# Wide matmuls in a two-layer and one-block transformer kernel: both halves of a feature tile in one pass of 512 columns

## The reference

```python
h = h + g1 * y                                    # y = even_mixer(...) @ w_out, or pool_mix(...)
hn = modulate(rms_norm(h, norm_ffn_g[layer]), sh2, sc2)
h = h + g2 * swiglu(hn, w1, w3, w2)               # hidden width 2816, two layers
...
x = x + mix @ w_out                               # second block, after DeltaNet and sparse attention
h2 = rmsnorm(x, norm_mlp)
x = x + jnp.square(jax.nn.relu(h2 @ w_up)) @ w_down   # hidden width 4096
```

## Time and profile before

| | |
|---|---|
| Median of three runs | 1388.35 us |
| Profiled execution, its own time | 1396.09 us |
| Its span | 1394.3 us |
| Mean granted TensorE clock | 0.945 |
| TensorE matmul busy | 1271.6 us (91%), 9480 records |
| TensorE weight load busy | 1180.4 us (85%), 9480 records |
| VectorE busy | 930.1 us (67%), 1562 records |
| ScalarE busy | 650.3 us (47%), 1163 records |
| GpSimd busy | 314.2 us (23%), 155 records |

### The profile page before, as it was taken

How to read it: one execution, slowest core, us unless ns; L and a number is a source line. 1 busy time by engine, 2 the same in 40 slices (tenths; PEclk the granted TensorE clock), 3 DMA queues, 4 the chain that set the end, 5 groups by cost and what they waited for, 6 DMA issues and landing times.

```text
span 1394.3 us, 22620 instructions
## 1 busy us (share of the span) xinstructions
PE 1271.6 (91%) x9480; PEld 1180.4 (85%) x9480; DVE 930.1 (67%) x1562; ACT 650.3 (47%) x1163; POOL 314.2 (23%) x155
## 2 busy tenths in 40 slices
PE   5679889999987999997997897988999999899999
PEld 1676679999976999996987775767999899899999
DVE  4956768998767665444476886777754576677543
ACT  2535746666545554433533445454322455465432
POOL 0241123433200100000732433331553530000000
PEclk9899999999989999996997998979999999999999
DMA  9642637888742656412351211112201265665530
GB/s 392 239 187 65 248 139 299 320 321 324 308 181 105 262 214 236 159 63 96 122 204 68 65 64 54 61 61 65 87 1 46 102 209 181 231 205 206 191 103 12
DMA packets 32358, 226.52 MB, mean 162 GB/s; under 512 B 3584, under 2 KB 4736, under 8 KB 5120
## 3 DMA queue, kind: packets, MB, share of 16 engines
q1 hardware_dynamic: 30528, 221.20, 42.9%
q10 hardware_dynamic: 1728, 3.87, 0.8%
HBM read 224.01 MB, written 1.05 MB: 161 GB/s over the span
## 4 chain that ended last, share of the span: by engine, by line
PE 73%; DVE 18%; ACT 7%; issue 1%; DMA 1%; POOL 0%; SPq 0%; DVEq 0%; POOLq 0%; ACTq 0%
PE bank L515 20%; PE bank L516 19%; PE bank L517 19%; PE bank L535 2%; ACT sb_whi L1140 2%; PE bank L1038 2%; PE bank L1025 2%; DVE sb_qk L2076 1%; DVE sb_tmp L1629 1%; DVE sb_bk L1923 1%; PE bank L1034 1%; ACT sb_ss L1423 1%; DVE sb_qk L2064 1%; DVE sb_qk L2088 1%; PE bank L820 1%
## 5 line engine op out<-in xcount | busy, mean ns | idle before, releaser
L515 PE MATMUL bank<-sb_xh,sb_whi 128*128 128x256 f32 x1544 | 453.5, 294 | 35.5 <-DVE sb_xl L1634 19.4
L516 PE MATMUL bank<-sb_xl,sb_whi 128*128 128x256 f32 x1544 | 442.6, 287 | 0.0
L517 PE MATMUL bank<-sb_xh,sb_wlo 128*128 128x256 f32 x1544 | 441.9, 286 | 0.0
L515 PEld LDWEIGHTS bank<-sb_xh,sb_whi 128*128 128x128 f32 x1544 | 303.3, 196 | 51.3 <-issue 19.0
L516 PEld LDWEIGHTS bank<-sb_xl,sb_whi 128*128 128x128 f32 x1544 | 304.4, 197 | 0.5 <-issue 0.2
L517 PEld LDWEIGHTS bank<-sb_xh,sb_wlo 128*128 128x128 f32 x1544 | 302.4, 196 | 0.0
L1140 ACT ACTIVATE sb_whi<-sb_ring 128x1024 fp32r<-128x1024 f32 (+1 forms) x201 | 210.5, 1050 | 92.6 <-PE bank L517 82.0
L1610 DVE TENSOR_TENSOR sb_wlo<-sb_ring,sb_whi 128x1024 fp32r<-128x1024 f32 x145 | 186.4, 1291 | 94.3 <-ACT sb_whi L1140 94.0
L2276 POOL TENSOR_TENSOR sb_wlo<-sb_ring,sb_whi 128x1024 fp32r<-128x1024 f32 x56 | 134.6, 2416 | 356.6 <-ACT sb_whi L1140 356.6
L1610 DVE TENSOR_TENSOR sb_wlo<-sb_more,sb_whi 128x1024 fp32r<-128x1024 f32 x108 | 145.2, 1352 | 72.6 <-ACT sb_whi L1140 72.3
L515 PE MATMUL bank<-sb_hh,sb_whi 128*128 128x256 f32 x608 | 174.2, 287 | 0.0
(11 more groups left out here) (337 smaller groups left out, 2247.5 us busy)
## 6 DMA issues: line engine op xcount, KB each, us to landing
sb_more<-in_w SPq DMA_DIRECT2D x34, 1024.0 KB, 5.3
sb_ring<-in_w SPq DMA_DIRECT2D x32, 1024.0 KB, 5.1
sb_ring<-in_adaT SPq DMA_DIRECT2D x26, 1024.0 KB, 7.2
sb_ring<-in_f SPq DMA_DIRECT2D x24, 1024.0 KB, 4.9
sb_more<-in_adaT SPq DMA_DIRECT2D x18, 1024.0 KB, 8.2
sb_ring<-in_gn SPq DMA_DIRECT2D x8, 1024.0 KB, 4.9
sb_ring<-in_gd SPq DMA_DIRECT2D x8, 1024.0 KB, 4.9
sb_ring<-in_up SPq DMA_DIRECT2D x8, 1024.0 KB, 4.9
```

The lines of the kernel that those rows point to most:

```text
L515: te.matmul(out, wh, rh, start=start, stop=False, skip_group_check=skip)
L516: te.matmul(out, wh, rl, start=False, stop=False, skip_group_check=skip)
L517: return te.matmul(out, wl, rh, start=False, stop=stop, skip_group_check=skip)
```

## The change

Each pair of high and low data becomes one tile in which the two halves of a feature tile lie side by side, 512 columns. The new helper `mm_wide` multiplies the high weights by both at once into the whole bank, and the low weights by the high data into its first 256 columns. So the bank holds two partial sums, and `residual` adds them to `h` one after the other, the second waiting for the first. The pool stage keeps its single one (`wide=False`). For every weight tile the wide matmul is issued first and the narrow one second; for the last weight tile of a group the order is turned round, so that the wide one ends it.

```diff
--- before.py
+++ after.py
@@ -361,16 +361,16 @@
         xcl = sb("xcl", [128, KT, T], F32R)
         kT = sb("kT", [128, 2, T])
         qT = sb("qT", [128, 4, T])
-        ah = sb("ah", [128, 8, T], F32R)
-        al = sb("al", [128, 8, T], F32R)
+        ahl = sb("ahl", [128, 8, 2, T], F32R)
+        ah, al = ahl[:, :, 0, :], ahl[:, :, 1, :]
         v0 = sb("v0", [128, 2, 2, 128])
         SBs = sb("SBs", [128, 10, T])
         PTs = ctxr[:, 0:6, :]
         close()
 
         scope()
-        hh = sb("hh", [128, NH0, T], F32R)
-        hl = sb("hl", [128, NH0, T], F32R)
+        hhl = sb("hhl", [128, NH0, 2, T], F32R)
+        hh, hl = hhl[:, :, 0, :], hhl[:, :, 1, :]
         more[1] = sb("more", [128, NEXTRA, SLOT])
         z8 = sb("z8", [128, 8, T])
         close()
@@ -420,8 +420,8 @@
         Msb = sb("Msb", [128, 4, 512])
         close()
         scope()
-        mxh = sb("mxh", [128, 8, T], F32R)
-        mxl = sb("mxl", [128, 8, T], F32R)
+        mxx = sb("mxx", [128, 8, 2, T], F32R)
+        mxh, mxl = mxx[:, :, 0, :], mxx[:, :, 1, :]
         odh = sb("odh", [128, 8, T], F32R)
         odl = sb("odl", [128, 8, T], F32R)
         close()
@@ -430,8 +430,8 @@
 
         scope()
         more[2] = sb("more2", [128, NEXTRA, SLOT])
-        hh2 = sb("hh2", [128, NH2, T], F32R)
-        hl2 = sb("hl2", [128, NH2, T], F32R)
+        hhl2 = sb("hhl2", [128, NH2, 2, T], F32R)
+        hh2, hl2 = hhl2[:, :, 0, :], hhl2[:, :, 1, :]
         close()
 
         def K(name, lo=0, hi=None):
@@ -515,6 +515,27 @@
                 te.matmul(out, wh, rh, start=start, stop=False, skip_group_check=skip)
                 te.matmul(out, wh, rl, start=False, stop=False, skip_group_check=skip)
                 return te.matmul(out, wl, rh, start=False, stop=stop, skip_group_check=skip)
+
+            def mm_wide(ps, wh, wl, r, first, last):
+
+                x = r.rearrange("p e t -> p (e t)")
+                if not last:
+                    te.matmul(ps[:, :], wh, x, start=first, stop=False, skip_group_check=True)
+                end = te.matmul(ps[:, 0:T], wl, r[:, 0, :], start=False, stop=last, skip_group_check=True)
+                if last:
+                    end = te.matmul(ps[:, :], wh, x, start=first, stop=True, skip_group_check=True)
+                return end
+
+            def product_wide(n, r, ready, ps):
+
+                _, hi, lo = unit_of(n)
+                P.wait_ge(*lo_done(n))
+                for k in range(KT):
+                    P.wait_ge(*dve.at(ready, k))
+                    c = slice(k * 128, (k + 1) * 128)
+                    end = mm_wide(ps, hi[:, c], lo[:, c], r[:, k, :, :], k == 0, k == KT - 1)
+                F.done(n)
+                return end
 
             def product(n, rh, rl, ready, out):
 
@@ -677,7 +698,7 @@
             for j in range(8):
                 u, _ = F.take("mixout")
                 ps = take(RG, ("mo", j), (dve, ("h", "ffn0", j)))
-                product(u, ah, al, "a", ps[:, 0:T]).then_inc(*pe.up(("mo", j), ("unit", u)))
+                product_wide(u, ahl, "a", ps).then_inc(*pe.up(("mo", j), ("unit", u)))
                 if j > 0:
                     mean_square("ffn0", j - 1)
             mean_square("ffn0", 7)
@@ -708,7 +729,7 @@
                             P.wait_ge(*lo_done(u))
                         P.wait_ge(*dve.at("hid", layer, k))
                         c = slice((n % 8) * 128, (n % 8 + 1) * 128)
-                        end = mm3(ps[:, 0:T], hi[:, c], lo[:, c], hh[:, k, :], hl[:, k, :], k == 0, k == NH0 - 1)
+                        end = mm_wide(ps, hi[:, c], lo[:, c], hhl[:, k, :, :], k == 0, k == NH0 - 1)
                         steps = [("unit", u)] * (n % 8 == 7) + [("down", layer, j)] * (k == NH0 - 1)
                         if steps:
                             end.then_inc(*pe.up(*steps))
@@ -1090,7 +1111,7 @@
             for j in range(8):
                 u, _ = F.take("wout2")
                 ps = take(RG, ("res", j), (dve, ("h", "mlp2", j)))
-                product(u, mxh, mxl, "mx", ps[:, 0:T]).then_inc(*pe.up(("res", j), ("unit", u)))
+                product_wide(u, mxx, "mx", ps).then_inc(*pe.up(("res", j), ("unit", u)))
                 if j > 0:
                     mean_square("mlp2", j - 1)
             mean_square("mlp2", 7)
@@ -1112,7 +1133,7 @@
                         P.wait_ge(*lo_done(u))
                     P.wait_ge(*dve.at("mhid", k))
                     c = slice((n % 8) * 128, (n % 8 + 1) * 128)
-                    end = mm3(ps[:, 0:T], hi[:, c], lo[:, c], hh2[:, k, :], hl2[:, k, :], k == 0, k == NH2 - 1)
+                    end = mm_wide(ps, hi[:, c], lo[:, c], hhl2[:, k, :, :], k == 0, k == NH2 - 1)
                     if n % 8 == 7:
                         end.then_inc(*pe.up(("unit", u), ("mdown", j)) if k == NH2 - 1 else pe.up(("unit", u)))
                         F.done(u)
@@ -1662,10 +1683,14 @@
             def scaled(i, gain, scale):
                 ve.scalar_tensor_tensor(scl[:, i, :], scale, 1.0, gain, ALU.add, ALU.mult).then_inc(*dve.up())
 
-            def residual(norm, j, step, gate):
-                V.wait_ge(*pe.at(step, j) if isinstance(step, str) else pe.at(*step, j))
-                ve.scalar_tensor_tensor(h[:, j, :], ps_of((step, j) if isinstance(step, str) else (*step, j))[:, 0:T], gate, h[:, j, :],
-                                        ALU.mult, ALU.add).then_inc(*dve.up(("h", norm, j)))
+            def residual(norm, j, step, gate, wide=True):
+
+                V.wait_ge(*pe.at(*step))
+                for e in range(1 + wide):
+                    if e:
+                        V.wait_ge(*dve.now())
+                    ve.scalar_tensor_tensor(h[:, j, :], ps_of(step)[:, e * T:(e + 1) * T], gate, h[:, j, :], ALU.mult, ALU.add).then_inc(
+                        *dve.up(*[("h", norm, j)] * (e == wide)))
 
 
             V.wait_ge(s_col, 16)
@@ -1775,7 +1800,7 @@
             for j in range(8):
                 weights("mixout")
                 V.wait_ge(*m2)
-                residual("ffn0", j, "mo", mods[:, 0, 16 + j:17 + j])
+                residual("ffn0", j, ("mo", j), mods[:, 0, 16 + j:17 + j])
             dve.note("layer0")
 
             def swiglu(layer, norm, after, i):
@@ -1817,7 +1842,7 @@
                             ada_later()
                         n += 1
                     V.wait_ge(*m3)
-                    residual(after, j, ("down", layer), mods[:, layer, 40 + j:41 + j])
+                    residual(after, j, ("down", layer, j), mods[:, layer, 40 + j:41 + j])
 
             V.wait_ge(*m2)
             scaled(2, C("nf", 0, 8), mods[:, 0, 32:40])
@@ -1835,7 +1860,7 @@
             c = F.raw("poolm")
             for j in range(8):
                 V.wait_ge(*dve.at("gcol"))
-                residual("ffn1", j, "pool", gcol[:, j:j + 1])
+                residual("ffn1", j, ("pool", j), gcol[:, j:j + 1], False)
             F.used(c)
             swiglu(1, "ffn1", "fin", 4)
             dve.note("block1")
@@ -2229,7 +2254,7 @@
             mixed(7)
             for j in range(8):
                 weights("wout2")
-                residual("mlp2", j, "res", 0.5)
+                residual("mlp2", j, ("res", j), 0.5)
             dve.note("block2")
 
 
@@ -2256,8 +2281,11 @@
             for j in range(8):
                 for k in range(4):
                     weights("down")
+                ps = ps_of(("mdown", j))
                 V.wait_ge(*pe.at("mdown", j))
-                ve.tensor_tensor(h[:, j, :], h[:, j, :], ps_of(("mdown", j))[:, 0:T], ALU.add).then_inc(*dve.up(("out", j)))
+                ve.tensor_tensor(h[:, j, :], h[:, j, :], ps[:, 0:T], ALU.add).then_inc(*dve.up())
+                V.wait_ge(*dve.now())
+                ve.tensor_tensor(h[:, j, :], h[:, j, :], ps[:, T:2 * T], ALU.add).then_inc(*dve.up(("out", j)))
 
         def gpsimd_program(gp):
             G, F = Waiter(gp), Flow()
```

## The result

| | before | after |
|---|---|---|
| Median | 1387.75 us (20 runs, 1381.32 to 1394.45) | 1393.39 us (20 runs, 1388.26 to 1401.8) |
| Ratio after to before | | 1.0044, 95% interval 1.0025 to 1.0062 |
| Profiled execution, span | 1396.09 us, 1394.3 us | 1388.26 us, 1386.5 us |
| Matmul records, VectorE instructions | 9480, 1562 | 8744, 1602 |

The change makes the kernel slower by 0.44%, some 6 us, where 7 us less was forecast. The two profiled executions stand the other way round. This is no contradiction: the executions of both kernels spread by 1%, and most of why they do is shown under experiment 8. So stages are compared here, not spans.

The account below looks back on a forecast made before the run. TensorE's stream of matmuls was taken to bound the kernel (73% of the chain). -16.4 (matmuls) + 1.5 (last tiles) + 3.1 (mixout) + 3.0 (wout2) + 1.5 (stall) = -7.3 us, from 1388.35 to 1381.0; range 1375 to 1391.

Parts of the forecast that it names:

- the cost of a triple: All changed contractions: the matmuls of one weight tile, 360 ns before in the last contraction, take 333 after, bounds 326 and 360.
- the term of the sum: Three long contractions: 27 ns saved on each of 608 weight tiles, 16.4 us gained.
- the 1.5 of the stall: First w2 contraction: TensorE waits because VectorE has too little time to spare; 1.5 us lost, bounds 0 and 4.8.
- the vector part: 40 residual tiles: a second dependent VectorE instruction adds 0.51 or 0.45 us each; mixout loses 3.1 us, wout2 3.0, last tiles 1.5.
- one ring of waits: Mixout: residual, ScalarE's square and copy, VectorE's low part, next residual; 3.06 us a turn becomes 3.57, exceeding TensorE's 3.09.
- The excess stays with each load or instruction: Rival, all triples: 13.3 ns twice, triple 347, gain 8.1 us, 1388 to 1389, no change; chance 0.22.
- the long float32 stream: Mixout's mean square: plain float32 records of 256 columns, 512 cycles, carry only about 2 ns beyond their columns.
- It decides from a triple of 347 upwards: Threshold for the slower rival: from there 608 x 13 no longer pays for the vector part, +7.6 us.
- The excess stays with the columns: Rival, all triples: a wide matmul costs 240 ns, triple stays 360, no tensor gain, +7.6 us, 1396; chance 0.10.

Follow-up runs that it names:

- experiment 8: Separate kernel, only fp32r matmuls with data and weights at shifted offsets: 256 columns took 120 ns at distance 0, 113 at 112 bytes.
- experiment 4: Separate kernel, only back-to-back fp32r matmuls in ten forms: three narrow 360 ns, wide and narrow 353; 512 columns alone 227, 256 alone 120.
- experiment 6: The changed kernel word for word, run once more: 1395.12 us, ratio 1.0068 to the kernel before.

## Why the prediction was wrong

**The step that failed** is the cost of a triple, "wide 216 ..., then narrow ... 117", sum 333. It is 353: the wide matmul costs 235 and not 216. I took it from a float32 record that streams for as many cycles, and took cycles for what counts. That record is one of two passes of a plain float32 matmul; a fp32r matmul of 512 columns by itself takes 227 (experiment 4). The narrow one, put at 117, was right at 118. What I had not seen is that at this place such a matmul carries 13 ns whether it has 256 or 512 columns, so that doubling its columns saves this once per weight tile at best, and 7 of the 13 are lost again when wide and narrow are taken in turn. Why is open. With 6.7 ns instead of 27, the term of the sum is -4.1 and not -16.4 us. Those 12.3 us, less the 1.5 of the stall and with 0.1 more in wout2, turn -7.3 into +3.6. The rest of the 6 us measured may in part be the long subtraction shown behind experiment 6, which the prediction did not have.

The Trainium skill gives, in "TensorE: Matmul & The Clock Gate" (section Back-to-back issue gap), columns over 2.4 GHz plus 2.5 ns for a single matmul by itself, and says that in a stream of loads and matmuls both set the spacing; the prediction used the formula without that limit, though its sum did not rest on it. The fp32r matmuls of this case each bring a load, and none keeps to that formula: 256 columns take 113 to 120 ns and not 109, 512 take 227 to 237 and not 216.

**Right to a hundredth of a microsecond a turn** was the vector part: 0.51 us a tile, turns of 3.57 and 3.45 where 3.57 and 3.44 were forecast, 3.1 us lost in mixout and 3.1 in wout2. The method was to follow one ring of waits through two queues, in four rows.

**The stall in the first w2 contraction**, 1.5 us, did not come; but neither did the speed that would have brought it.

**The rivals.** "The excess stays with each load or instruction" was the nearest in mechanism: it named 13.3 ns and 347. It was given 0.22, because of the long float32 stream that keeps only 2 ns, the very row that misled the forecast. "It decides from a triple of 347 upwards" holds: at 353 the kernel came out slower. "The excess stays with the columns" named the right sign, and at 1396 came nearest to the measured time, by luck: it rests on a triple of 360. My argument against it, that "up" reads operands of the same shape at 113, was the thread to pull: the same form at 113 and at 120 in one kernel, and I went on without asking what differs. It was the address.

**The clock** played no part in the turns of mixout. The windows from the first to the last residual, of the kernel before and of the one after, columns as in the earlier trace rows:

```profile
173.70:196.60 22.90, 22.78 (x182) 22.06 (x181) 12.50 (x16) 9.58 (x14) 4.07 (x2) 1.00 0.10 40
```

```profile
171.00:196.50 25.50, 23.45 (x126) 19.39 (x125) 15.20 (x22) 9.56 (x14) 3.10 (x2) 1.00 0.08 34
```

TensorE now stands idle in each turn of the ring, and the granted clock is 1.00 all the same. Elsewhere it moves single executions. In run 6 a stretch of the first product stage was at the 1.2 GHz level, where the first changed run had 33 matmuls in the same window at 1.00:

```profile
214.40:217.80 3.40, 3.29 (x15) 3.29 (x16) 2.28 (x3) 2.17 (x2) 0.00 (x0) 0.50 0.73 304
```

That is some 1.7 us, and no part of the change.

## What to carry to other kernels

A price has to come from the same form of instruction, in the order in which it will be issued; where no row has that form, the range must reach to the price by instruction. Where one form runs at two paces in one kernel, find out what differs before anything is built on either; here the place of the data against the weights was worth 15 us, and the wide matmul 4. And count the followers of an instruction on a queue: half a microsecond on VectorE was free in three stages, but for the last tile, and stood in the time of two, where a ring of waits was 0.2 to 0.3 us short of TensorE's turn.

## What the runs showed of the hardware

- Matmuls in fp32r, each with its own load, carry 13.3 ns beyond columns at 2.4 GHz, at 256, 384 and 512 columns alike, when data and weights begin at the same place modulo 256 bytes and the weights have 128 columns. With 32 columns of weights it is 18 ns at 512 and 11 at 256. Wide and narrow in turn carry 6.7 ns more a pair (353.4); two and two, four and four, eight and eight take 348.3, 350.8 and 349.2.
- The pace of 256 columns hangs on the distance between the two in the partition modulo 256 bytes: 120 ns at 0, 113 at 112 and at 192. Only the distance counts: with both moved by 64, 128 or 192 bytes it was 120 again. For 512 columns it is 227 at 0 and 229 to 237 elsewhere.
- At the distance 192 there are two paces, 113.3 and 117.8 ns, steady until something else comes between, and different between stages and runs of one program. With `xh` and `xl` at 112 bytes six runs stayed within 0.14%, where the 23 of before differ by 1.2%. What chooses the pace is open.
- A subtraction of 128x1024 on VectorE, 1.23 us alone, gets longer when it begins under a GpSimd tensor_tensor of 128x1024: to 1.74, 2.21, 2.56 and 2.91 us in four profiles, where the two overlap by 0.66, 1.13, 1.48 and 1.83. The added time is the overlap less 0.15 us in each.
